# Mixture-of-experts block: the fourth up block loaded in two transfers, the activation in three VectorE operations, half of the scatter moved behind the third up block

## The reference, cut to what matters

```python
gt = jnp.minimum(xb @ w_gate[e] + b_gate[e], SWIGLU_LIMIT)                  # limit 7.0
up = jnp.clip(xb @ w_up[e] + b_up[e], -SWIGLU_LIMIT, SWIGLU_LIMIT)
hid = gt * jax.nn.sigmoid(SWIGLU_ALPHA * gt) * (up + 1.0)                   # alpha 1.702
return hid @ w_down[e] + b_down[e]
```

## Time and profile before

| | |
|---|---|
| median of 3 runs | 1481.98 us (1480.98 to 1482.08) |
| profiled execution, its own time | 1481.4 us |
| span of its trace | 1479.6 us |
| stretch of the experts in the trace | 120 to 1027 us |
| granted TensorE clock, mean | 0.997 |
| TensorE busy | 1396.9 us, 94% of the span |
| moved by DMA | 491.38 MB |

### The profile page before, as it was taken

The page is one execution under the profiler, slowest core; times in us unless marked ns, Lnnn a source line. Parts: engine busy times, 40 slices in busy tenths (PEclk is TensorE's granted clock), DMA queues, the critical chain, the costliest instruction groups (busy, mean ns, idle before and its releaser), DMA issues.

```text
span 1479.6 us, 23681 instructions
## 1 busy us (share of the span) xinstructions
PE 1396.9 (94%) x10102; PEld 782.3 (53%) x10102; DVE 535.5 (36%) x980; ACT 341.9 (23%) x504; POOL 90.2 (6%) x44
## 2 busy tenths in 40 slices
PE   8989999999999999899889998998999999999998
PEld 6544333333333333333333333333979988899997
DVE  1763121121111111121112111212989658777766
ACT  0531011010100010010001000102765543444442
POOL 0000000000000000000000000002000050132232
PEclk9998999999999999999999999999999999999999
DMA  9699999999999999999999999999544114255552
GB/s 362 241 396 367 426 429 426 430 427 429 428 428 428 428 429 427 430 427 429 425 429 427 430 427 428 429 427 407 179 144 143 62 56 158 86 198 185 182 187 85
DMA packets 45125, 491.38 MB, mean 332 GB/s; under 512 B 5008, under 2 KB 5520, under 8 KB 13488
## 3 DMA queue, kind: packets, MB, share of 16 engines
q1 hardware_dynamic: 44928, 490.48, 80.7%
q10 hardware_dynamic: 144, 0.13, 0.0%
HBM read 489.54 MB, written 1.05 MB: 332 GB/s over the span
## 4 chain that ended last, share of the span: by engine, by line
PE 66%; DMA 28%; DVE 3%; ACT 2%; issue 1%; SPq 0%; DVEq 0%; ACTq 0%
DMA ring<-in_w_exp 20%; PE bank L831 16%; PE bank L860 10%; PE bank L891 8%; PE bank L892 8%; PE bank L893 8%; DMA work<-in_w_exp 5%; DMA spare<-in_w_exp 3%; PE bank L789 3%; PE bank L777 2%; PE bank L726 2%; PE bank L647 1%; PE bank L677 1%; PE bank L797 1%; ACT spare L1480 1%; PE bank L851 1%
## 5 line engine op out<-in xcount | busy, mean ns | idle before, releaser
L831 PE MATMUL bank<-ring,spare 128*64 128x512 f32 x1344 | 302.2, 596 | 25.0 <-DMA ring<-in_w_exp 25.0
L2013 DVE TENSOR_SCALAR work<-bank 128x512 f32<-128x512 f32 x32 | 22.1, 692 | 741.0 <-PE bank L831 741.0
L831 PEld LDWEIGHTS bank<-ring,spare 128*64 128x64 f32 x1344 | 92.9, 136 | 220.7 <-issue 160.2
L860 PE MATMUL bank<-ring,spare 128*64 128x512 f32 x672 | 148.8, 595 | 14.7 <-ACT spare L1480 14.7
L892 PE MATMUL bank<-work_parts,ring_parts 128*128 128x256 f32 x568 | 159.3, 281 | 0.0
L1476 ACT ACTIVATE work<-work 128x512 f32<-128x512 f32 x32 | 20.2, 631 | 535.7 <-DVE work L2013 535.7
L831 PE MATMUL bank<-work,spare 128*64 128x512 f32 x576 | 129.7, 595 | 8.3 <-DMA work<-in_w_exp 8.3
L892 PEld LDWEIGHTS bank<-work_parts,ring_parts 128*128 128x128 f32 x568 | 107.7, 190 | 1.1
L860 PEld LDWEIGHTS bank<-ring,spare 128*64 128x64 f32 x672 | 46.9, 137 | 103.1 <-issue 90.3
L891 PE MATMUL bank<-hn_hi,ring_parts 128*128 128x256 f32 x352 | 99.3, 282 | 0.0
L893 PE MATMUL bank<-hn_hi,ring_parts 128*128 128x256 f32 x352 | 99.0, 281 | 0.0
(11 more groups left out here) (467 smaller groups left out, 1979.1 us busy)
## 6 DMA issues: line engine op xcount, KB each, us to landing
ring<-in_w_exp SPq DMA_DIRECT2D x126, 2048.0 KB, 34.6
work<-in_w_exp SPq DMA_DIRECT2D x54, 2048.0 KB, 34.6
spare<-in_w_exp SPq DMA_DIRECT2D x12, 2048.0 KB, 31.6
ring<-in_ffn_up SPq DMA_DIRECT2D x22, 1024.0 KB, 4.8
ring<-in_ffn_down SPq DMA_DIRECT2D x22, 512.0 KB, 3.4
ring<-in_w_in SPq DMA_DIRECT2D x2, 2048.0 KB, 17.2
ring<-in_w_out SPq DMA_DIRECT2D x4, 1024.0 KB, 16.6
ring<-in_w_k SPq DMA_DIRECT2D x4, 1024.0 KB, 16.9
```

The source lines that it names most:

```text
L831: ins = pe.matmul(to[n2 * CAP:(n2 + 1) * CAP, :], x_e[:, 2 * j + kk, :], w[:, b, kk, n2 * BANK:(n2 + 1) * BANK], start=False, stop=j == UP ...
L860: ins = pe.matmul(y_bank[n2 * CAP:(n2 + 1) * CAP, :], hidT[:, k % 4, k // 4 * CAP:(k // 4 + 1) * CAP], w[:, kk, n2 * BANK:(n2 + 1) * BANK] ...
L2013: dve.tensor_scalar(gt, bank[4][:, :], LIMIT, None, ALU.min).then_inc(gt_ready, 1)
```

## The change

Four edits, one diff.

1. The fourth up block of each expert (load 3 of six) is issued as two transfers of 128 x 8 KB, each with a semaphore of its own; the first halves come with `slot_in`, the second with semaphores reused from the start of the kernel. So that one half serves whole rows of the product, the up blocks are laid out slice first (`k b n` for `b k n`), on the host and in `up_slot`. TensorE waits for the second half between the two slices. The source of a half is 8 KB out of every 16 KB.
2. The activation has three operations of VectorE. The bias of the up half has 1 added once, by GpSimd at the start, ahead of ScalarE's first cast; the clip is then to 1 - 7 and 1 + 7. ScalarE computes the sigmoid straight from the gate bank, and both the gate (at 7) and the sigmoid (at its value for 7) are clipped in the products.
3. `scatter(1)` stands behind the third up block.
4. The transposes of `hid` stand ahead of those of the placement matrix.

```diff
+PIECES = lambda load: 2 if load % SLOTS == UP_SLOTS - 1 else 1
+
+def seconds_of(ring_order, s, loads):
+    return sum(PIECES(load) - 1 for load in range(loads) if ring_order[load % len(ring_order)] == s)
...
+SIGMOID_LIMIT = float(1.0 / (1.0 + np.exp(-SWIGLU_ALPHA * LIMIT)))
...
+        second_in = {1: (w_in_in[0], 32), 3: (w_in_in[1], 32), 5: (w_in_in[2], 32), 7: (w_in_in[3], 32), 8: (w_g_in, 16)}
...
         def up_slot(s):
-            return slot_area(s).rearrange("p (b k n) -> p b k n", b=2, k=2)
+            return slot_area(s).rearrange("p (k b n) -> p b k n", b=2, k=2)
...
             def load_slot(s, e, j):
-                sp.dma_start(slot_area(s), expert_slot(e, j)).then_inc(slot_in[s], 16)
+                w = SLOT // PIECES(j)
+                for i in range(PIECES(j)):
+                    cols = slice(i * w, (i + 1) * w)
+                    sp.dma_start(slot_area(s)[:, cols], expert_slot(e, j, cols)).then_inc(second_in[s][0] if i else slot_in[s], 16)
...
+                def second_landed(j):
+                    load = turn * SLOTS + j
+                    s = ring_order[load % len(ring_order)]
+                    per_turn, ahead = seconds_of(ring_order, s, turns * SLOTS), seconds_of(ring_order, s, load)
+                    if base:
+                        ahead += FIRST_LOOPS * seconds_of(FIRST_RING, s, FIRST_TURN * SLOTS)
+                    pe.wait_ge(second_in[s][0], pe.snap(it * (per_turn * 16) + (second_in[s][1] + (ahead + 1) * 16)))
...
                     for kk in range(2):
+                        if kk and PIECES(j) == 2:
+                            second_landed(j)
...
                     if j == 1:
                         pe.wait_ge(y_ready, now)
                         scatter(0, False)
+                    if j == 2:
+                        scatter(1, False)
 
                 pe.wait_ge(place_ready, ahead)
                 gather()
-                scatter(1, False)
                 add_bias(y_bank, 2 * D, False)
+                pe.wait_ge(hid_ready, now)
+                for j in range(4):
+                    ins = pe.transpose(gate_bank[:, j * P:(j + 1) * P], hid[:, j * P:(j + 1) * P], ident)
+                ins.then_inc(hidT_done, 1)
                 pe.wait_ge(uc_ready, now)
                 pe.wait_ge(place_g_ready, now)
                 for t in range(TT):
                     ins = pe.transpose(up_bank[:, t * P:(t + 1) * P], place_g[:, t, :], ident)
                 ins.then_inc(place_T_done, 1)
-
-                pe.wait_ge(hid_ready, now)
-                for j in range(4):
-                    ins = pe.transpose(gate_bank[:, j * P:(j + 1) * P], hid[:, j * P:(j + 1) * P], ident)
-                ins.then_inc(hidT_done, 1)
...
-            act.wait_ge(bias_in, 16)
+            act.wait_ge(gt_ready, 1)
...
-                act.wait_ge(gt_ready, now)
-                act.activation(sg, gt, ACT.Sigmoid, scale=SWIGLU_ALPHA).then_inc(sg_ready, 1)
+                act.wait_ge(slots_used, act.snap(it * (turns * SLOTS) + ((base + turn) * SLOTS + UP_SLOTS)))
+                act.activation(sg, bank[4][:, :], ACT.Sigmoid, scale=SWIGLU_ALPHA).then_inc(sg_ready, 1)
...
-                dve.tensor_scalar(gt, bank[4][:, :], LIMIT, None, ALU.min).then_inc(gt_ready, 1)
-                dve.tensor_scalar(uc, bank[5][:, :], LIMIT, -LIMIT, ALU.min, ALU.max).then_inc(uc_ready, 1)
+                dve.tensor_scalar(uc, bank[5][:, :], 1.0 + LIMIT, 1.0 - LIMIT, ALU.min, ALU.max).then_inc(uc_ready, 1)
                 dve.wait_ge(uc_ready, now)
-                dve.wait_ge(gt_ready, now)
-                dve.scalar_tensor_tensor(out=vv, in0=uc, scalar=1.0, in1=gt, op0=ALU.add, op1=ALU.mult).then_inc(vv_ready, 1)
                 dve.wait_ge(sg_ready, now)
+                dve.scalar_tensor_tensor(out=vv, in0=bank[4][:, :], scalar=LIMIT, in1=uc, op0=ALU.min, op1=ALU.mult).then_inc(vv_ready, 1)
                 dve.wait_ge(vv_ready, now)
-                dve.tensor_tensor(hid, vv, sg, ALU.mult).then_inc(hid_ready, 1)
+                dve.scalar_tensor_tensor(out=hid, in0=sg, scalar=SIGMOID_LIMIT, in1=vv, op0=ALU.min, op1=ALU.mult).then_inc(hid_ready, 1)
...
         def _(pool):
+            pool.wait_ge(bias_in, 16)
+            pool.tensor_scalar(bias_all[0:BIAS_ROWS, D:2 * D], bias_all[0:BIAS_ROWS, D:2 * D], 1.0, None, ALU.add).then_inc(gt_ready, 1)
...
-    ups = ups.transpose(0, 1, 4, 2, 3, 5).reshape(NE, UP_SLOTS, P, SLOT)
+    ups = ups.transpose(0, 1, 4, 3, 2, 5).reshape(NE, UP_SLOTS, P, SLOT)
```

More of the change, by code:

```diff
@@ L488, in program, with expert_slot @@
         ffn_done, out_ready = sem("ffn_done"), [sem(f"out_ready{t}") for t in range(TT)]
+        second_in = {1: (w_in_in[0], 32), 3: (w_in_in[1], 32), 5: (w_in_in[2], 32), 7: (w_in_in[3], 32), 8: (w_g_in, 16)}
         block = ctx.enter_context(nc.Block())
-        def expert_slot(e, j):
-            return A["w_exp"][bass.ds(e, 1), j, :, :].rearrange("o p n -> p (o n)")
+        def expert_slot(e, j, cols):
+            return A["w_exp"][bass.ds(e, 1), j, :, cols].rearrange("o p n -> p (o n)")
         def slot_area(s):
```

## The result

The changed kernel takes 1483.65 us (median of 20 runs, 1480.57 to 1485.11) against 1481.20 us (20 runs, 1477.51 to 1482.08). The ratio is 1.0016, 95% interval 1.0010 to 1.0021: 1.5 to 3.1 us later. Forecast was +0.4 us and a range of 1479.5 to 1486.0, so the number holds and the sum behind it does not: 2 us of it are to be found. The kernel before is also 0.8 us faster over 20 runs than over the three that the forecast stood on (1481.98), which brings 1483.65 nearer to 1482.4 than the shift of 2.45 us is to 0.4.

A forecast was written before the change was run, and what follows sets the result against it. The loads' pace, 29.37 us per expert, was taken to bound the experts. Terms: -1.1 (tail) + 1.5 (loads) = +0.4, on the median 1482.0 giving 1482.4 us; range 1479.5 to 1486.

The forecast's parts named there:

- What bounds the kernel: Over the experts: loads keep one pace, 29.37 us per expert; TensorE alone would need 26.9 and is held from about 500 us.
- The tail: Last expert: down blocks start about 11.85 us behind the third up block's start instead of 12.96, with 0.3 wait for hid.
- 1.5 us lost: Experts' loads: split halves take 2.47 us per MiB against 2.447, a difference of 0.023 over 64 MiB.
- the shorter rows at 416 GB/s: Stretch from 28 to 38 us with shorter rows mixed in: 2.52 us per MiB, an upper bound of 4.7 us lost.
- The fixed 2 us per transfer: Skill page's fixed cost per DMA, 64 us over 32 added transfers; the forecast held that the full queue leaves no room.
- 1.1 us gained: Last expert: down blocks start at 1018.0 against 1019.10, a gain counted once and in full in the end time.
- half rows cost more than their likeness says: Rival at the queue of loads: a split load costs more than forecast; at 416 GB/s +3.6 us, 1485.6; chance 0.15.
- point of decision: Extra cost per split load above which the change is slower: 1.1 / 32 = 0.034 us.
- visible bound: Extra cost per split load above which the change is visibly slower: (3.0 + 1.1) / 32 = 0.13 us.
- The experts that TensorE paces: First fourteen experts: scatter only moves, -0.3 to +0.3 us per expert, period 26.6 to 27.2, covered by the loads.
- The bias on GpSimd: Start of the kernel: adding 1 to the bias takes 0 to 2.15 us; price 0, about 2 us without slack.
- the slack of 0.85: Start of the kernel: VectorE's 0.85 us idle before L1900, to take up a subtraction starting 0.25 late.

The follow-up runs named there:

- e9: Kernel before with only scatter(1) moved behind the third up block; one execution, 1477.1 us.
- e10: Kernel before with only the three-operation activation (1 added to the bias by GpSimd at the start); one execution, period 26.88 us where TensorE sets the pace.
- e2: Changed kernel with the fourth up block as one whole transfer again; ratio to the kernel before 0.9998 (0.9987 to 1.0009).
- e1: Kernel before with only the fourth up block split into two transfers of 8 KB rows; ratio to the kernel before 1.0017 (1.0006 to 1.0027).
- e5: Changed kernel with the fourth up block whole and the layer norm rows loaded behind in_w_lora; ratio to the kernel before 0.9996 (0.9987 to 1.0005).
- e11: As e5, but the placement transposes stand ahead of those of hid again; ratio 1.0003 (0.9994 to 1.0013).
- e12: The kernel of e5 run once more to narrow its interval; ratio 0.9991 (0.9980 to 1.0002).
- e3: Changed kernel with the two halves of the fourth up block each contiguous in HBM; one execution, period 29.444 us.
- e4: Changed kernel with the fourth up block as one 2 MiB transfer in 256 rows of 8 KB; one execution, period 29.459 us.
- e6: Changed kernel with the layer norm rows loaded behind in_w_lora; ratio 1.0007 (0.9998 to 1.0016).
- e7: As e2, but all six loads of an expert in rows of 8 KB, one transfer each; one execution, 1492.0 us.
- e8: Changed kernel with the fourth up block in two transfers of 64 partitions, rows of 16 KB; one execution, 1869 us.

## Why the prediction was right in its number and wrong in its sum

*What bounds the kernel: right.* e9 and e10 change TensorE's pace by +1 and by 0 us per expert, and the last experts still come when their loads come. The first experts pass at 27.26 us in place of 26.88, and e2, which has the same, ends with no loss that its interval can tell. Two totals were read short, without harm to the argument: SyncE waits for an area 444.2 us behind the up blocks and 314.9 more behind the down blocks, and TensorE waits for landings 36.3 us in 54 places, not 25.0 in 37 (the views list the areas apart).

*The tail: right.* 11.88 us against a forecast 11.85, 0.38 us of wait for hid against 0.3. How I shared it out, 0.25 for the split and the rest for the scatter, holds only in that order: the split alone gains 1.47 us (e1), and the other three edits on top of it take 0.39 back, since the scatter no longer stands over the activation.

*The step that failed first: "1.5 us lost" for the loads.* The mechanism was right (rows of 8 KB cost more, in a queue that is never empty) and so was the sign; the term was mis-sized. I read 2.47 against 2.447 us per MiB from landing times given to 0.1 us. The seven periods of the two traces gave 0.087 us per split load, 29.369 against 29.456. All the traces together give less and leave no doubt about it. Periods are over the last seven experts; the last column is the time in which each trace's DMA packets add up from 60 to 420 MB, 28.6 experts of weights (worked out from the packets, no view prints it).

| loads | traces | period, us | 360 MB, us |
|---|---|---|---|
| all whole, rows of 16 KB | before, e2, e5, e10, e11, e12 (last column also e9) | 29.361 to 29.383, mean 29.373 | 840.8 to 841.0 |
| fourth up block in rows of 8 KB | changed, e1, e3, e4, e6 | 29.434 to 29.459, mean 29.448 | 842.9 to 843.1 |
| all six in rows of 8 KB | e7 | 29.817 | 853.8 |

So a split load costs 0.075 us, in place of 0.047 forecast, and 32 of them 2.4 us in place of 1.5. All six cost 0.444 us, 5.9 times as much by the periods and 6.1 times by the last column: the price goes with the number of rows, 9 to 9.5 ns for each row that is added on its DMA engine, whatever the number of transfers (e4) or the gap between rows (e3). Only rows of 8 and 16 KB were tried. The error of 1.5 is the reading's: 0.1 us over two transfers is 0.05 per MiB, twice the difference sought. The row just beside it, the shorter rows at 416 GB/s, had bounded it at 4.7. The Trainium skill's page "DMA: Bandwidth & Descriptors", section "Bandwidth", has about 10.5 ns per packet. That is close in number, but it is another quantity, the shortest time of one 4 KB transfer divided by its 64 packets, and it neither confirms nor contradicts the price of a large row here. The fixed 2 us per transfer that I set against the trace is what the Trainium skill's page "DMA: Bandwidth & Descriptors", section "Anatomy of one DMA", gives for transfers issued by GpSimd; SyncE issues these. As a price in this full queue it is nowhere: e4 and the changed kernel differ by 32 transfers and 0.003 us per expert, less than the five traces of the second row differ among themselves (0.025).

*The step that was missing: "1.1 us gained" was carried to the end of the kernel.* I followed the tail to the down blocks and stopped. What is late next is GpSimd's work on `in_w_lora`, whose start is set by the landing behind the experts' loads. VectorE's subtraction reads two SBUF tiles, and stands still while GpSimd works. Shown by e5 against e2: the same two subtractions in 1.02 us with GpSimd done, and 1.98 us beside it. The first of the two takes 0.68 us alone (e5); in the kernel before, e2, the changed kernel and e1 it starts 0.25, 1.10, 1.41 and 1.78 us ahead of GpSimd's end, and in all four it ends 0.54 to 0.55 us behind that end. The Trainium skill's page "SBUF — State Buffer", section "SBUF: two separate sides", states such a lock for a VectorE operation with two SBUF inputs against a GpSimd operation that reads SBUF, the later one waiting for the whole of the earlier; the trace agrees: the first subtraction of the changed kernel ends 0.54 us behind GpSimd's end.

The corrected sum is +2.4 for the rows and 0 for the tail, +2.4, against 2.45 measured (1.5 to 3.1). Both errors, 1.1 at the tail and 0.9 in the rows, point the same way. The number came out within its range because the range was wide, 6.5 us, and not because the sum was right.

*The rival "half rows cost more than their likeness says"* was what happened, at 0.075 us per load, above its point of decision (0.034) and below its visible bound (0.13). Alone it would give +1.3 us with the gain at the tail, less than was measured; the lost tail belongs to it. *The experts that TensorE paces*: forecast 26.6 to 27.2, measured 27.26. I had missed that a scatter between two blocks costs 0.15 us more than behind them (the two blocks took 7.02 us together, now 3.58 and 3.59).

*The bias on GpSimd*: no delay at the end of the start, as forecast, but the operation takes 2.77 us, above the end of my bounds (2.15). Timeline of the changed kernel:

```profile
68.40 2.77 POOL L2601 TENSOR_SCALAR work<-work 96x1024 f32<-96x1024 f32 x1 [67.95 <-DMA work<-in_bias]
```

The copy at L1923, in the changed kernel, starts at 84.36 with no idle time before it; in the kernel before, it starts at 84.86 behind 0.85 us of waiting for TensorE. VectorE's operation beside GpSimd's (L1906, 68.57 us) took 3.01 us; it was 2.28 before. These 0.73 us, and not ScalarE's later cast, took up almost all of the slack of 0.85. The copy comes 0.5 us earlier, like what stands ahead of it.

## What to carry to other kernels

Where the DMA engines never pause, count rows before anything else: splitting a load that already has 16 KB rows buys an earlier start once and pays for it in every load. A gain at the end of a stage has to be followed to the next thing that doesn't start from it, here a landing and the engine that works on it; moving one transfer in the queue (e5) brought 0.96 us up to the first product of the next block, a whole operation of VectorE less (e10) brought nothing. And to find a price of 1.5% of a load, divide a long run of periods, in several executions, not the difference of two landings: the landings gave 0.047 us, one pair of traces 0.087, all of them 0.075.

## What the runs showed of the hardware that I had not expected

*TensorE's clock and short pauses.* In e9 TensorE pauses twice in each expert for 0.68 us (for hid and for ScalarE's copy). In 7 of 31 periods the down blocks then ran at the lower level. Stretches of e9:

```profile
193.00:194.00 1.00, 0.82 (x4) 0.22 (x6) 0.06 (x1) 0.13 (x1) 0.00 (x0) 0.67 1.00 426
194.00:195.00 1.00, 1.00 (x6) 0.39 (x4) 0.00 (x0) 0.00 (x0) 0.00 (x0) 0.50 1.04 442
```

0.50 is 1.2 GHz of 2.4; each such expert took 1.69 us longer. With both pauses shorter (0.38 and 0.46 us, the changed kernel) or one of them gone (0.68 us once, the kernel before) none did. e3, with the pauses of the changed kernel, had one fall to the lower level, behind a wait of 2.56 us for a load at 709 us.

*The spread of the runs.* The clock ahead of the experts (0.63 to 1.00 at 106 to 120 us) moves the first refill between 120.5 and 124.5 us from one execution to another, whatever the kernel. In e1 the clock fell once more behind the experts (0.86 at 1036 to 1048 us, 1.00 in all the others) and cost 1.0 us. The largest part stands further on. For the first 150 us behind the first product the traces agree to 0.1 us (e1 apart, and e9 and e6 to 0.3), but the last 1390 matmuls, most of them in the feed-forward layer, take 198.6 us in five of them (e3, e6, e7, e9, e12) and 200.9 to 201.2 in the other nine. Between 1300 and 1450 us TensorE is busy without a pause at a granted clock of 1.00; its 128x256 matmuls there have a mean of 274 to 278 ns in e12 and 282 in e5, which are the same kernel. So this is not the edits' doing, it is as large as the whole effect, and its cause is open. Differences of 1 us drown in it unless they are read inside the trace.

*64 partitions.* In e8 one load of six in each expert goes in two transfers over 64 partitions. From 200 to 1100 us the loads ran at 303 GB/s with the DMA engines 99% busy, and an expert took 42.8 us (mean of 21 periods) in place of 29.4: 13.4 us more for a load of 2 MiB, which takes a sixth of the 29.4 otherwise. The Trainium skill's page "SBUF — State Buffer", section "Door 1: The DMA port swizzle", says that a transfer over 64 partitions reaches half of the ports, at about 218 GB/s. By that the load would take 9.6 us in place of 4.9 and the expert 34.1 (an estimate from the page). The direction agrees, the size is short by a factor of three. What else slows the queue is open.
